# One PSUM bank and nine orders in a two-block transformer kernel

## The reference, cut to what matters

```python
proj = rmsnorm(h, norm_mix_g) @ w_in
fq, fk, fv, ff, gq, gf, gi, gg = jnp.split(proj, split_idx, axis=-1)
log_f = jax.nn.log_sigmoid(ff + fox_f_bias)
fox_out = fox_attention(heads(fq), heads(fk), heads(fv), log_f)   # logit[t,s] += F[t] - F[s]
rec = rmsnorm(hgrn2_chunkwise(gq, gf, gi, lbs), hgrn_norm_g) * jax.nn.silu(gg)
h = h + concat([fox_out, rec]) @ w_out
h = h + memory_cross_attention(rmsnorm(h, norm_x_g), mem_n, w_xq, w_xkv, w_xo)
h = h + jnp.square(jax.nn.relu(rmsnorm(h, norm_ff_g) @ w1)) @ w2
```

```python
y_attn = (rms_norm(diff_attention(q_d, k_d, v_d, lam), subln_g) * (1 - lam_init)) @ w_attn_branch
y_pool = (einsum('bsgc,gcd->bsgd', window_means_minus_token(u_p), pool_w) * pool_scale) @ w_pool_branch
y_mem = memory_cross_attention_2(q_m, rms_norm(mem, norm_mem), w_mem_kv) @ w_mem_branch
x = x + rms_norm((gates[0]*y_attn + gates[1]*y_pool + gates[2]*y_mem) @ w_out, norm_mix_post)
up = causal_depthwise_conv(rms_norm(x, norm_ffn_pre) @ w_up, conv_w, conv_b)
x = x + rms_norm((gelu(g) * v) @ w_down, norm_ffn_post)
```

## Time and profile before

| | |
|---|---|
| median of three runs | 907.87 us (906.85 to 908.96) |
| the profiled execution's own time | 906.91 us |
| its span, first to last instruction | 905.1 us |
| TensorE busy | 890.8 us |
| VectorE busy | 605.0 us |
| ScalarE busy | 489.3 us |
| GpSimd busy | 107.6 us |
| mean granted TensorE clock | 1.000 |

### The profile page before, as it was taken

One profiled execution on the slowest core, in us unless ns is written; L12 is line 12 of the kernel. 1 busy time (PEld: TensorE's weight loads), 2 busy tenths in 40 slices (PEclk: granted clock), 3 DMA queues, 4 the chain that ended last, 5 costly groups with the idle time before them and its releaser, 6 DMA issues.

```text
span 905.1 us, 15854 instructions
## 1 busy us (share of the span) xinstructions
PE 890.8 (98%) x6305; PEld 820.6 (91%) x6305; DVE 605.0 (67%) x812; ACT 489.3 (54%) x727; POOL 107.6 (12%) x136
## 2 busy tenths in 40 slices
PE   9999999899999999999999999999999999999997
PEld 8988987788988999988899989999999899999886
DVE  6795875755655766644467547898686688888643
ACT  7766545534655655433364336664644666666432
POOL 6431132200000100000026070001000100000000
PEclk9999999999999999999999999999999999999999
DMA  9958632234533866555547554345556486666641
GB/s 290 304 176 278 213 124 94 94 135 144 187 94 94 262 200 202 194 186 189 199 149 224 199 196 150 105 146 158 187 186 186 117 226 192 185 187 203 213 140 47
DMA packets 135266, 159.63 MB, mean 176 GB/s; under 512 B 3951, under 2 KB 113773, under 8 KB 134957
## 3 DMA queue, kind: packets, MB, share of 16 engines
q1 hardware_dynamic: 133261, 151.79, 52.4%
q0 software_dynamic: 1344, 6.03, 1.9%
q10 hardware_dynamic: 608, 1.06, 0.3%
HBM read 157.81 MB, written 1.05 MB: 176 GB/s over the span
## 4 chain that ended last, share of the span: by engine, by line
PE 86%; DVE 5%; ACT 3%; issue 3%; DMA 1%; SPq 1%; POOL 0%; DVEq 0%; POOLq 0%; ACTq 0%
PE tb L698 15%; PE tb L700 15%; PE tb L699 15%; PE acc L698 11%; PE acc L700 11%; PE acc L699 11%; DMA raw<-in_w_in 1%; PE acc L990 1%; ACT whi L1327 1%; DVE wlo L1863 1%; DVE wlo L1939 1%; PE tb L1084 0%; DVE dz L2017 0%; PE acc L1210 0%; PE tb L1066 0%
## 5 line engine op out<-in xcount | busy, mean ns | idle before, releaser
L1863 DVE TENSOR_TENSOR wlo<-raw,whi 128x2048 fp32r<-128x2048 f32 x138 | 317.1, 2301 | 187.6 <-ACT whi L1327 187.2
L1327 ACT ACTIVATE whi<-raw 128x2048 fp32r<-128x2048 f32 x138 | 264.1, 1915 | 183.9 <-PE acc L700 121.5
L698 PE MATMUL tb<-xhi,whi 128*128 128x256 f32 x1192 | 331.8, 278 | 2.1 <-DVEq L2002 1.2
L700 PE MATMUL tb<-xhi,wlo 128*128 128x256 f32 x1192 | 329.3, 276 | 0.0
L699 PE MATMUL tb<-xlo,whi 128*128 128x256 f32 x1192 | 329.3, 276 | 0.0
L698 PEld LDWEIGHTS tb<-xhi,whi 128*128 128x128 f32 x1192 | 223.8, 188 | 3.0 <-DVEq L2002 1.4
L699 PEld LDWEIGHTS tb<-xlo,whi 128*128 128x128 f32 x1192 | 223.9, 188 | 0.1
L700 PEld LDWEIGHTS tb<-xhi,wlo 128*128 128x128 f32 x1192 | 223.8, 188 | 0.0
L698 PE MATMUL acc<-whi,hid_hi 128*128 128x512 f32 x128 | 50.0, 390 | 0.0
L700 PE MATMUL acc<-whi,hid_lo 128*128 128x512 f32 x128 | 49.8, 389 | 0.0
L699 PE MATMUL acc<-wlo,hid_hi 128*128 128x512 f32 x128 | 49.8, 389 | 0.0
(11 more groups left out here) (408 smaller groups left out, 1524.2 us busy)
## 6 DMA issues: line engine op xcount, KB each, us to landing
raw<-in_w_in SPq DMA_DIRECT2D x37, 1024.0 KB, 5.2
raw<-in_w SPq DMA_DIRECT2D x32, 1024.0 KB, 5.4
raw<-in_w_up SPq DMA_DIRECT2D x44, 512.0 KB, 5.0
raw<-in_w_down SPq DMA_DIRECT2D x22, 512.0 KB, 4.1
raw<-in_w_xkv SPq DMA_DIRECT2D x8, 1024.0 KB, 6.3
raw<-in_w_out SPq DMA_DIRECT2D x8, 1024.0 KB, 4.9
raw<-in_w_mem_kv SPq DMA_DIRECT2D x4, 1024.0 KB, 5.1
raw<-in_w_xq SPq DMA_DIRECT2D x4, 1024.0 KB, 5.0
```

The source lines that it names most:

```text
L698: pe.matmul(o, a_hi, b_hi, start=start, stop=False)
L700: return pe.matmul(o, a_lo, b_hi, start=False, stop=stop)
L1327: act.activation(whi[:, n % RING, :m], raw[:, n % RING, :m], ACT.Copy).then_inc(hi_ready, 1)
L1863: dve.tensor_tensor(low(n), raw[:, n % RING, :m], whi[:, n % RING, :m].bitcast(F32), ALU.subtract).then_inc(lo_ready, 1)
```

## The change

It changes where nine pieces of work stand in the engines' streams, one PSUM bank, and which engine does one copy. No other work is added or removed.
- Slab 6 goes to bank 3 instead of 1 and waits for the constants' copy instead of for ff; slab 8 waits for ff's bank. ScalarE empties fq and makes the high part of slab 8 before the forget gate's Exp and Ln, and VectorE makes the low part of slab 8 before the scans.
- In the attention loop at i = 5 ScalarE copies head 4's turned probabilities and makes the high part of slab 23 ahead of emptying the values; at i = 7 it does head 6's copy, laid (2,3), the Exp of head 7 and of level 8 and head 6's high part first. TensorE's wait for xv's second half at i = 7 goes. VectorE does head 7's mask first, and the low part of slab 25 last.
- vm's second tile is emptied by VectorE, beside ScalarE's first, with a semaphore `vm_low`.
- The first token tile's half of cross_out(1) is issued before the values of heads 2 and 3.
- `plo` is made one group per turn, i = 3 to 6.
- `summed("h4", 1)` stands after one pair of h4's low parts instead of two.

```diff
-        X_BANK = {0: 0, 1: 1, 2: 2, 3: 0, 4: 1, 5: 0, 6: 1, 7: 0, 8: 1}
-        BANK_BEFORE = {3: 0, 4: 1, 5: 3, 6: 4, 7: 5, 8: 6}
+        X_BANK = {0: 0, 1: 1, 2: 2, 3: 0, 4: 1, 5: 0, 6: 3, 7: 0, 8: 1}
+        BANK_BEFORE = {3: 0, 4: 1, 5: 3, 7: 5, 8: 4}
...
-            def row_slab(n, hi, lo, k0, nk_all):
+            def row_slab(n, hi, lo, k0, nk_all, tiles=(0, 1)):
...
-                for t in range(TT):
+                for t in tiles:
...
-                last.then_inc(slab_done, 1)
+                if tiles[-1]:
+                    last.then_inc(slab_done, 1)
...
+                if n == 6:
+                    pe.wait_ge(cols_ready, 2)
...
-            pe.wait_ge(cols_ready, 2)
...
                         emptied(first["xk"] + 3)
-                        emptied(first["xv"] + 3)
                         spread("mem2", tb[:, 1 - first["km"] % 2, :])
...
             emptied(first["vm"] + 1)
+            pe.wait_ge(vm_low, 1)
...
             cross_transpose(3)
+            row_slab(first["xo"] + 1, chi, clo, 2, 8, (0,))
             cross_values(2)
             cross_values(3)
-            cross_out(1)
+            row_slab(first["xo"] + 1, chi, clo, 2, 8, (1,))
             cross_out(2)
...
             hi(first["ff"] + RING)
+            n = first["fq"]
+            empty_pair(n, fqT[:, 0, :], fqT[:, 1, :], 0.125)
+            hi(n + RING)
...
             act.wait_ge(cols_ready, 2)
-            n = first["fq"]
-            empty_pair(n, fqT[:, 0, :], fqT[:, 1, :], 0.125)
-            hi(n + RING)
...
+                if i in (5, 7):
+                    fox_copy(i - 1)
+                if i == 5:
+                    hi(n + RING)
                 if i == 7:
-                    fox_copy(6)
+                    laid(turned_mem, C["norm_mem_2"], (2, 3))
+                    fox_exp(7)
+                    hg_exp(8)
+                    fox_hi(6)
...
                     if i == 7:
-                        laid(turned_mem, C["norm_mem_2"], (2, 3))
                         act.wait_ge(spread_made, 3)
...
-                    empty(n, vm[:, 0, :], ACT.Copy, acc[:, 0, 0, :], scale=rs[:, NORM["mem2"], 0:1])
-                    act.activation(vm[:, 1, :], acc[:, 0, 1, :], ACT.Copy, scale=rs[:, NORM["mem2"], 1:2])\
-                        .then_inc(act_emptied, 1)
+                    empty(n, vm[:, 0, :], ACT.Copy, acc[:, 0, 0, :], scale=rs[:, NORM["mem2"], 0:1]).then_inc(act_emptied, 1)
...
-                hi(n + RING)
-                if i < 8:
-                    if 0 < i < 7:
+                if i != 5:
+                    hi(n + RING)
+                if i < 7:
+                    if i not in (0, 5):
                         fox_copy(i - 1)
-                    if i == 7:
-                        hg_exp(8)
...
             lo(first["ff"] + RING)
 
+            lo(first["fq"] + RING)
             dve.memset(dz[:, 1, 0:P], 0.0)
...
-            lo(first["fq"] + RING)
             lo(first["fq"] + 1 + RING)
...
-                if i == 7:
-                    laid(turned_mem, C["norm_mem_2"], (2, 3), 4)
-                lo(n + RING)
-                if i == 7:
-                    hg_diff(8)
+                if i not in (7, 11):
+                    lo(n + RING)
                 if i < 8:
                     fox_mask(i)
+                    if i == 7:
+                        laid(turned_mem, C["norm_mem_2"], (2, 3), 4)
+                        hg_diff(8)
...
                     fox_norm(i)
                     hg_merge(i)
+                    if i == 7:
+                        lo(n + RING)
...
                 elif i == 11:
+                    dve.wait_ge(slab_done, n + 1)
+                    dve.tensor_scalar(vm[:, 1, :], acc[:, 0, 1, :], rs[:, NORM["mem2"], 1:2], None, ALU.mult).then_inc(vm_low, 1)
+                    lo(n + RING)
...
-                if i == 3:
-                    dve.wait_ge(pl["hi"], 1)
-                    for g in range(4):
+                if 3 <= i <= 6:
+                    if i == 3:
+                        dve.wait_ge(pl["hi"], 1)
+                    for g in (i - 3,):
...
-                    last.then_inc(pl["lo"], 1)
+                    if i == 6:
+                        last.then_inc(pl["lo"], 1)
...
-            h4_lo(0, (0, 1))
+            h4_lo(0, (0,))
             summed("h4", 1)
+            h4_lo(0, (1,))
             diagonal(1)
```

More of the change, by code:

```diff
@@ L254, in two_blocks @@
         act_link, dve_link, pool_link = sem("act_link"), sem("dve_link"), sem("pool_link")
-        warm_ready = sem("warm_ready")
+        warm_ready, vm_low = sem("warm_ready"), sem("vm_low")
         consts_ready, cols_t, cols_ready, lam_ready, lb_ready = (
```

## The result

The changed kernel takes 900.5 us (median of 4 executions, 900.04 to 901.04) against 907.94 us (4 executions, 906.85 to 908.96): a ratio of 0.9921, 95% interval 0.9906 to 0.9936. So 7.4 us are won where 5.8 were forecast, and the time lies 0.5 us under the lower end of the range, 901.0. The two profiled executions tell another story: 906.91 became 901.04 and the span went from 905.1 to 899.3, 5.8 us, close to the sum of the prediction's terms, 5.7. What has to be explained first is therefore not a stage of the kernel. It is the 1.5 us that the medians show and the pair of profiles does not.

The account below looks back on a forecast made before the run. TensorE, busy 98%, bounds the kernel; only its eleven waits can be won. 1.0 + 3.2 + 0.5 + 0.35 + 0.39 + 0.24 = 5.7 us gives 901.2 from the profiled 906.91, 902.2 from the median; forecast 902.1, range 901.0 to 904.4.

Parts of the forecast that it names:

- from 901.2 to 902.2: Last step of the sum: 901.2 us by the profiled execution, 902.2 by the median of the runs, 0.96 higher.
- the 1.9 of head 7's wait: Attention loop, slab 23: TensorE's 1.76 us wait for p of head 7 goes, plus 0.17; bounds 0.7 and 1.9.
- the third: Rival: VectorE's and GpSimd's operations miss each other at 41 us, merge 7 is early; 6.4 to 7.5 won; chance 0.06.
- Queries, 1.0: Slabs 5 to 10: waits of slabs 6 and 8 go, partly given back; 1.0 us won, bounds 0.6 and 1.7.
- the link that I had named, slab 10: Query slabs: slab 10's low part ends at 63.1, the slab would like 62.7; 0.4 us given back.
- Attention loop, 3.2: i=5 to 8, slabs 20 to 23: five waits go or shrink, 0.27 + 0.16 + 0.78 + 1.9 + 0.1; bounds 2.0 and 3.6.
- a second meeting with GpSimd: Between head 7's mask and p: one meeting with GpSimd's product (0.4 us) was counted, a second could come.
- rival 2: p of head 7 still late, half or all of 1.9 comes back; 3.0 to 4.7 us won; chance 0.22.
- The other four, 1.48: Memory values 0.5, cross values 0.35, pool remainders 0.39, h4 0.24 us won.
- slab 21 and cross_out(2): Sign: the prediction is wrong if either waits; slab 21's bank had 0.3 us of cover.
- Rivals 4 and 5: 4: waits turn up at next gates, under 1.8 us won, chance 0.06. 5: merge 8 late, kernel slower, 0.04.
- Merge 8: Attention loop, queued behind p: done at 182.0, wanted at slab 24's end, 183.6; cover 1.6 us.

Follow-up runs that it names:

- right-hand column: No edit: executions sorted by mean granted clock, those at 0.998 or more; median span 904.7 us for the kernel before (30 executions), 898.8 for the kernel after (10).

## Why the prediction was right and wrong

**What failed.** The step is the one in the sum that goes from 901.2 to 902.2: the profiled execution "lies 0.96 below the median of the runs shown", and I carried the 0.96 over as if it were a property of measuring. It was part of what the change removes. The profiled execution was one of the right-hand column, and more than half of the others (35 of 65 by their mean clock) are some 1.8 us longer; in the profiles with a fall in the attention loop it costs 1.5 to 1.6. In the terms of the sum it is the 1.9 of head 7's wait that was too small: I priced the wait by its length, and the clock behind it at nothing. In an execution with the fall the two together are worth about 3.5. I had read "mean granted TensorE clock 1.000" in the profile and three times that reach from 906.85 to 908.96, and had not asked whether the 1.76 us wait does something in the other executions that it does not do in this one. No rival had it: the third, "more than I say", holds the time that came, 900.5, but gives it to GpSimd's multiply and an early merge, neither of which came about. The fall explains the 1.3 us between 5.9 and 7.2. The 0.2 that are left to 7.4 are within the spread of the four executions of each kernel.

Two readings in the prediction are wrong without moving the forecast. The eleven waits of the earlier trace rows sum to 6.89 us and not to 6.69. And the last matmul starts at 899.22 us, so some 5.5 us of the span lie behind it and not 10.

**Queries, 1.0.** Alone the part can't be told from nothing in the timing (its interval allows 1.0 us of gain). A single pair of profiles gives this term badly, since slab 6's wait hangs on the start: it is between 0.29 and 1.46 in the profiles of kernels with the old bank. From the slab behind the constants' transposes to head 0's transposes, those eight profiles take 73.9 to 75.1 us, 74.6 in the middle; the kernel after and the one with this part alone take 73.5 to 73.6 in their three profiles. So it is about 1.0, between 0.4 and 1.5, as forecast. The mechanism is as told: slab 6 unlisted, a new wait of 0.63 at slab 7. The multiply hit the forget arithmetic harder than I charged. GpSimd's timeline of the kernel after:

```profile
41.32 1.30 POOL L615 TENSOR_TENSOR fqT<-fqT,fs 128x512 f32<-128x512 f32 x1 [6.36 <-ACT fqT L1419]
```

VectorE's timeline of the same kernel, the same moment and the low part of slab 10:

```profile
41.32 1.44 DVE L2009 TENSOR_SCALAR am<-am,small 8x256 f32<-8x256 f32 x1
...
61.37 2.29 DVE L1869 TENSOR_TENSOR wlo<-raw,whi 128x2048 fp32r<-128x2048 f32 x1
```

The same scaling took 0.34 in the earlier trace rows. It is held 1.1 us; I had charged 0.4 to 0.5. The Trainium skill, page "SBUF — State Buffer", section "SBUF: two separate sides", gives the shared port as an exclusive lock for a whole instruction, and this row agrees with it, more plainly than the meeting of the earlier trace rows. What I had not seen is that the same multiply already stood in this chain in the kernel before, beside the scans. Its timelines of VectorE and GpSimd:

```profile
46.53 3.71 DVE L2017 TENSOR_TENSOR_SCAN dz<-bb,dz 128x128 f32<-128x128 f32 x8
...
46.76 1.29 POOL L615 TENSOR_TENSOR fqT<-fqT,fs 128x512 f32<-128x512 f32 x1 [11.64 <-ACT fqT L1416]
```

In the kernel after the scans have no multiply beside them and take 2.63. So the 1.1 us lost at the forget arithmetic, which slab 7 waits for, are won again ahead of slab 10. Later multiplies now stand beside the copy behind the scans (L2027, 1.60 us instead of 0.69) and beside L2040 (1.98 instead of 0.85), which the prediction did not have, and no longer beside a small subtraction (1.15 before, 0.16 after). What gives the gain back is the link that I had named, slab 10: its low part ends at 63.66, and TensorE's timeline has the slab right behind it, with 0.47 instead of the usual 0.23 between two matmuls and no wait in the listing, because the modelled length of the matmul before covers most of it:

```profile
63.33 0.40 PE L700 MATMUL acc<-whi,xlo 128*128 128x512 f32 x1
63.80 0.47 PE L698 MATMUL acc<-whi,xhi 128*128 128x512 f32 x1
```

With the multiply held the same slab starts at 63.46, 0.15 behind its low part too, and with the low parts first it does not wait.

**Attention loop, 3.2.** 3.5 in the pair of profiles, and 3.45 with the part alone, the clock not counted. The mask of head 7 stands first, `laid` and the difference behind it, and p is in time. I expected a second meeting with GpSimd as possible; it came. VectorE's timeline of a second profile of the kernel after:

```profile
166.01 0.54 DVE L2088 TENSOR_TENSOR fs<-tb,causal 128x384 f32<-128x384 f32 x1
...
171.58 0.63 DVE L2096 TENSOR_SCALAR fs<-fs,rden 128x128 f32<-128x128 f32 x1
172.14 1.40 DVE L2097 TENSOR_SCALAR fs<-fs,rden 128x256 f32<-128x256 f32 x1
```

Both scalings are held by GpSimd's two products, which stand there from 170.84 to 173.39. Still p is ready at 173.5, and TensorE comes to it at 174.02: 0.5 us of margin, where I had 0.2. So rival 2, that half of the 1.9 comes back, had its meetings in the profile and not their price. The chain from mask to p is 7.5 us (166.01 to 173.54), where I had summed 7.6.

**The other four, 1.48.** 1.64 in the profiles and 1.7 by the medians of the run with them alone. vm's second copy, cross_out(1) in halves and `plo` in four turns leave no listed wait, and slab 21 and cross_out(2) wait for nothing; the pool's turns do not hand the wait on. h4 keeps 0.64 where 0.6 was said, because ScalarE's last square is late and not the sum behind it: its read ends at 710.64 and the sum (L2432) starts at 710.67.

**Rivals 4 and 5.** That each wait turns up again at the next gate is right in one place of ten, slab 7's, with slab 10's behind it, which is listed when slab 7's is cleared. Merge 8 was not late: in the second profile of the kernel after VectorE's copy ends at 179.97 and TensorE reads it at 181.79, 1.8 us later, where I had counted 1.6.

## What to carry to other kernels

Before a profile is used for a median, compare its mean granted clock with that of the other executions: a single profile can belong to the half that does not pay for a stall. Leave out what the clock does behind the last matmul. A stall among small matmuls can have two prices, as here: its own length and, in some executions, the clock behind it. Filling it with idle work buys back the second only, and here that was too little for the timing alone to tell from nothing. Count a gain from the last place that the change can't have moved: the start alone shifts a pair of executions by up to a microsecond. When an order is mended, follow the engine's chain to the gate where it next has slack; here that was slab 10, and not slab 7, whose wait the listing shows.

## What the runs showed of the hardware

I had not expected that the same kernel, with waits in the loop that agree to 0.01 us, has its clock fall in one execution and not in the next (35 of 65 by the mean clock), nor that it can fall 2 us behind a wait of only 0.22 us in front of sixteen 64-column products; whether that wait, those products or something before them brings it is not tested. In the four profiles with a fall it went to 1.2 GHz, lasted three to four microseconds and cost 1.5 to 1.6 us. Why it comes in one execution and not in another is not settled. Nor had I expected an operation on 8 partitions and 256 columns to be held for 1.1 us by another engine's multiply on other data.
